# Both low halves of each table block of the first product-key pass on GpSimd, and a larger selection budget per block

## The reference, cut to what matters

```python
def _peer(hn, w_query, sub_keys, expert_down, expert_up):
    q = (hn @ w_query).reshape(b, s, PEER_HEADS, 2, PEER_QUERY_DIM // 2)
    sc = jnp.einsum('bshcd,hckd->bshck', q, sub_keys)
    v1, i1 = lax.top_k(sc[..., 0, :], 16)
    v2, i2 = lax.top_k(sc[..., 1, :], 16)
    cand = (v1[..., :, None] + v2[..., None, :]).reshape(b, s, 8, 256)
    cidx = (i1[..., :, None] * 128 + i2[..., None, :]).reshape(b, s, 8, 256)
    top, pos = lax.top_k(cand, 16)
    idx = jnp.take_along_axis(cidx, pos, axis=-1)
    gate = jax.nn.softmax(top, axis=-1)
    ...
        act = gelu(hb . expert_down[ib]);  out = (gate * act) . expert_up[ib]
```

## Time and profile before

| | |
|---|---|
| median of 3 runs | 4505.56 us (4504.31 to 4511.51) |
| the profiled execution | 4504.23 us, its span 4502.3 us |
| busy in the span | PE 4045.6 us (90%), DVE 3031.9 (67%), ACT 2273.7 (51%), POOL 1127.2 (25%) |
| first pass, by TensorE | 3318.5 to 3955.9 us |
| second pass, by TensorE | 3959.5 to 4497.9 us |
| HBM | 1001.57 MB read, 77.97 MB written |

### The profile page before, as it was taken

One profiled execution on the slowest core, in us unless ns is written; L12 is line 12 of the kernel. 1 busy time (PEld: TensorE's weight loads), 2 busy tenths in 40 slices (PEclk: granted clock), 3 DMA queues, 4 the chain that ended last, 5 costly groups with the idle time before them and its releaser, 6 DMA issues. The chain is left out here.

```text
span 4502.3 us, 60232 instructions
## 1 busy us (share of the span) xinstructions
PE 4045.6 (90%) x22760; PEld 3230.1 (72%) x22760; DVE 3031.9 (67%) x3742; ACT 2273.7 (51%) x2916; POOL 1127.2 (25%) x547
## 2 busy tenths in 40 slices
PE   6797769999999999999699779789879999999999
PEld 6785646666555655555479777678779999988787
DVE  5254468888888888888446342254489877788884
ACT  3332146676676666677335235322335989533332
POOL 2121100000000000000122222132224555666662
PEclk9898879999999999999799889899889999999999
DMA  2222269999999999999423321232236999999995
GB/s 87 66 67 78 69 241 343 362 367 366 363 366 349 364 366 365 364 369 355 151 88 101 137 79 63 91 103 71 89 135 214 318 348 348 355 357 373 355 344 189
DMA packets 506172, 1082.32 MB, mean 240 GB/s; under 512 B 23570, under 2 KB 209170, under 8 KB 494712
## 3 DMA queue, kind: packets, MB, share of 16 engines
q1 hardware_dynamic: 465416, 936.49, 58.4%
q0 software_dynamic: 40560, 143.16, 8.7%
HBM read 1001.57 MB, written 77.97 MB: 240 GB/s over the span
## 5 line engine op out<-in xcount | busy, mean ns | idle before, releaser
L1627 DVE TENSOR_TENSOR ffn_low<-moe_expert_raw,moe_expert_high 128x2048 fp32r<-128x2048 f32 (+1 forms) x576 | 1189.8, 2110 | 255.7 <-ACT moe_expert_high L1580 255.7
L1580 ACT CAST moe_expert_high<-moe_expert_raw 128x2048 fp32r<-128x2048 f32 x570 | 976.0, 1764 | 420.0 <-DMA moe_expert_raw<-in_w_gate 137.3
L2876 ACT CAST peer_high<-peer_raw 128x1024 fp32r<-128x1024 f32 x256 | 256.2, 1050 | 443.4 <-PE peer_ps L2858 265.8
L1473 POOL DMA_INDIRECT scratch_h<-ffn_result,ffn_y_rows x16 | 46.3, 2896 | 1340.7 <-DVE ffn_result L1619 1340.7
L298 PE MATMUL peer_ps<-peerbuf_hnT_high,peer_high 128*128 128x384 f32 x1024 | 353.2, 345 | 27.2 <-DVE peer_low L2682 23.5
L299 PE MATMUL peer_ps<-peerbuf_hnT_high,peer_low 128*128 128x384 f32 x1024 | 344.3, 336 | 0.0
L300 PE MATMUL peer_ps<-peerbuf_hnT_low,peer_high 128*128 128x384 f32 x1024 | 344.2, 336 | 0.0
L2682 DVE TENSOR_TENSOR peer_low<-peer_raw,peer_high 128x1024 fp32r<-128x1024 f32 x192 | 257.0, 1366 | 102.6 <-ACT peer_high L2876 102.2
L298 PE MATMUL ffn_gate_p<-moe_expert_high,ffn_x_high 128*66 128x512 f32 (+1 forms) x768 | 290.2, 378 | 18.8 <-DVE ffn_low L1627 18.8
L298 PE MATMUL ffn_up_p<-moe_expert_high,ffn_x_high 128*66 128x512 f32 (+1 forms) x768 | 288.4, 376 | 5.8 <-DVE ffn_low L1627 5.8
L298 PE MATMUL ffn_down_p<-moe_expert_high,ffn_t_high 128*66 128x512 f32 x704 | 279.4, 397 | 12.5 <-DVE ffn_low L1627 12.5
(11 more groups left out here) (523 smaller groups left out, 10021.9 us busy)
## 6 DMA issues: line engine op xcount, KB each, us to landing
moe_expert_raw<-in_w_gate SPq DMA_DIRECT2D x80, 2048.0 KB, 9.6
moe_expert_raw<-in_w_up SPq DMA_DIRECT2D x80, 2048.0 KB, 9.9
moe_expert_raw<-in_w_down SPq DMA_DIRECT2D x80, 2048.0 KB, 10.7
peer_raw<-in_peer_down_t SPq DMA_DIRECT2D x64, 1024.0 KB
peer_raw<-in_peer_up_t SPq DMA_DIRECT2D x64, 1024.0 KB
scratch_a<-peer_gelu SPq DMA_DIRECT2D x64, 384.0 KB
scratch_g<-peer_spread SPq DMA_DIRECT2D x24, 1024.0 KB
peer_spread<-scratch_g SPq DMA_DIRECT2D x16, 1536.0 KB, 12.3
```

What stands on the lines that cost most here:

```text
L1473: pool.indirect_dma_start(h_dram, bass.IndirectOffsetOnAxis(ap=y_rows[:, 0:1], axis=0), result[:, :], None, compute_op=ALU.add).then_inc(y ...
L1580: act.copy(half_of(high, q, h), half_of(raw, q, h)).then_inc(high_done, 1)
L1627: dve.tensor_tensor(half_of(low, q, h), half_of(raw, q, h), half_of(high, q, h).bitcast(F32), ALU.subtract).then_inc(low_done, 1)
L2876: act.copy(high[:, q % 2, cols], raw[:, q % PR_RAW, cols]).then_inc(high_done, 1)
```

## The change

GpSimd makes both low halves of the blocks of the first pass, and DVE none; the semaphores are counted accordingly (`low_done_pool` counts every half of the first pass, `low_done` those of the second). The budget of a block goes from 6.0 to 7.2, which puts more selection pieces in each block and everything behind them in earlier blocks. The second pass has the same instructions.

```diff
@@ -2487,7 +2487,7 @@
     for b in range(PEER_BLOCKS):
-        budget, many = 6.0, 0
+        budget, many = 7.2, 0
@@ -2684,8 +2684,10 @@
         def lows_made(engine, q):
-            engine.wait_ge(low_done, q + 1 if q < PAIRS else PAIRS + 2 * (q - PAIRS + 1))
-            engine.wait_ge(low_done_pool, min(q + 1, PAIRS))
+            if q < PAIRS:
+                engine.wait_ge(low_done_pool, 2 * (q + 1))
+            else:
+                engine.wait_ge(low_done, 2 * (q - PAIRS + 1))
@@ -2778,8 +2780,8 @@
                 for q in range(PEER_BLOCKS):
-                    if q < PAIRS:
-                        low_half(pool, q, 1).then_inc(low_done_pool, 1)
+                    for half in (0, 1) if q < PAIRS else ():
+                        low_half(pool, q, half).then_inc(low_done_pool, 1)
@@ -2824,7 +2826,7 @@
                         pe.wait_ge(high_done, tile + 1)
-                        pe.wait_ge(low_done if j == 0 else low_done_pool, q + 1)
+                        pe.wait_ge(low_done_pool, tile + 1)
@@ -2936,7 +2938,7 @@
                 for q in range(PEER_BLOCKS):
-                    for half in range(1 if q < PAIRS else 2):
+                    for half in (0, 1) if q >= PAIRS else ():
                         low_half(dve, q, half).then_inc(low_done, 1)
```

## The result

| | before | after |
|---|---|---|
| median | 4505.54 us | 4535.46 us (4531.78 to 4541.3, 4 runs) |
| ratio | | 1.0068 (95% interval 1.0053 to 1.0083) |
| span of the profiled execution | 4502.3 us | 4539.5 us |
| first pass, first to last matmul | 637.4 us | 671.4 us |
| second pass | 538.5 us | 537.6 us |

The change makes the kernel slower by 0.7%, more than my range held (4499 to 4534) and more than twice what I forecast (+13). The 34.0 us in the first pass are nearly the whole of it. Of the 37 us between the two profiles, 2.5 lie ahead of the pass, in code that is the same (DVE's last search step there ends that much later), and 1.1 between that step and the first matmul, which waits for a low half that now takes GpSimd 2.4 us and took DVE 1.2. The runs' medians differ by 30.

The account below looks back on a forecast made before the run. The prediction took DVE to bound the first pass for 190 us and TensorE for 449 us. From 4504.23 us, +4 up to and behind the last one-hot wait, +11 in the tail and -1 in the second pass gave 4518 us, range 4499 to 4534.

Parts of the forecast that it names:

- the last coupled group is 0.9: First pass: the last one-hot group TensorE waits for is 0.9 in block 15, where it was 0.11 in block 19.
- The break-even at 154.4: First pass: group 0.9 ready 154.4 us after the first matmul, with 483.0 us of TensorE work behind it, would break even.
- DVE starts sooner: Start of the first pass: DVE begins with a selection step at about 3309.0 instead of waiting 8.6 us for a cast.
- The stalls, 20 us: DVE up to group 0.9: held up 20 us in all by GpSimd's low halves, ends 9 and 27 us.
- TensorE is free from there: First pass behind group 0.9: DVE's remaining work fits beside some 7 us of TensorE work, so TensorE waits no more.
- Term 2: Tail of the first pass, from block 51: GpSimd needs 10.0 us a block against TensorE's 8.32 and becomes the bound; +11 us.
- Term 3: Second pass: fewer accumulations and an earlier end of full DMA load shorten TensorE's waits; -1 us (-5 to +3).
- B: Rival, first pass: faster, the end of the selection decides alone and stalls stay at 9 us; 4496 us, chance 0.13.
- C: Rival: gathers wait for dots and dots for DMA rows, a ring that delays GpSimd's low halves; 4536 us, chance 0.12.

Follow-up runs that it names:

- e6: The changed kernel with at most two groups in each block up to block 21 (before: three in blocks 16, 18, 20): 4530.64 us, ratio 1.0049.
- e7: The kernel before with GpSimd making both low halves in blocks 0 and 1 alone, budget 6.0: 4504.78 us, ratio 0.9990.
- e5: The changed kernel with GpSimd's half 0 cut to one column instead of 1024 in blocks 2 to 16: 4518.21 us, ratio 1.0024.
- e3: The changed kernel with one wait more: GpSimd waits for the end of half 0 before it begins half 1: 4537.71 us, ratio 1.0067.
- e2: The kernel before with the budget alone raised to 7.2, DVE keeping half 0 of every first-pass block: 4555.99 us, ratio 1.0108.
- e4: The changed kernel with GpSimd making both halves only in blocks 0 to 16, DVE half 0 from block 17: 4530.94 us, ratio 1.0057.

## Why the prediction was wrong

- **That the last coupled group is 0.9**: right. It came at 173.9 us. The break-even at 154.4 took TensorE to be free for the 483.0 us behind it; they were 497.5, and 488.2 in e6.
- **DVE starts sooner**: right. Its first instruction follows the stage before by 0.5 us instead of 8.6. TensorE's first low half comes 1.1 us later, which I had left out. e7 shows that this is worth something only because DVE has no low half left in its order.
- **The stalls, 20 us**: the step that failed. They were 35.7, above my upper end of 27 too. I took a rate per low half (0.63 to 0.79 us) from the old schedule and multiplied it by the new number. The mechanism was right, the rate wasn't: it changes with the schedule, 0.8 us a low half before, 1.1 after, 1.8 with the larger budget alone. The error moves the one-hot by 15.7 us. e5 shows the mechanism by itself: 15 low halves less are 20 us less stall, 19.9 us on the one-hot and 17 us of time. That the low halves come in pairs isn't what made the rate too low: e3 takes the pairs apart and keeps the stall, e2 has no pairs and the highest rate.
- **"TensorE is free from there"**: wrong, a second step. I had seen that ScalarE was within 2 us of DVE, and didn't carry it past the selection. 5.2 us of waits and the slow clock behind them; e6: 7.2 us of the pass in blocks 16 to 21.
- **Term 2, the tail, +11 us**: the mechanism was right, the size wrong. GpSimd's pairs there stand 9.3 to 9.6 us apart (five blocks from 3935.94 to 3982.33, and from 3871.87 to 3919.93), where I had 10.0, and the first accumulations are two rows in block 57 and not three, so TensorE was idle six times, 3.8 us together, 5.4 with the slow restarts; e4: 4.8.
- **Term 3, -1 us**: -0.9 in the profile, which confirms nothing: the second pass takes 533.2 to 540.6 us in the profiles of e4 and e6, with the same instructions.
- **Rivals**: B needed half the stall rate and got more than the old one. C named the right size for a wrong reason, so its hit is luck: no ring through the gathers shows after block 20, DVE and DMA had time there. What I had not asked is what each of the two edits does alone. The larger budget was to me a consequence of the move; it was the costly one (e2).

Sum of the pass: 19.5 on the one-hot, 5.4 in the tail, and the 9.1 left of 34.0 between them.

What stays open: what sets the rate of the stall, and so why e3's sum didn't fall although the waits were cut in two, and why e2's is highest; whether a GpSimd low half can be placed under the search or a reduction at all times, which would cost nothing by these rows, wasn't tried. The longest single wait, the first for a group (10.50 us at 3434.23), I did not take apart further.

## What to carry to other kernels

When two engines share work, it isn't only the load that an engine loses that counts, but what it then waits for: 23 us of low halves left DVE and 20 us of stall came back. A stall rate read from one schedule doesn't carry over to another. Fixed work that bounds a stretch leaves TensorE time for other work beside it; packing it into fewer blocks (here four fewer, 33 us of TensorE) hardly shortens that work and leaves more for afterwards. A planner's parity (here two or three groups in the block behind the selection) was worth 7 us of the pass. Each edit should be costed alone before their sum.

## What the runs showed of the hardware

A DVE instruction with two SBUF inputs that meets a GpSimd low half waits for it, and can wait for two that run back to back: 7.04 us for one of 2.29 us, twice, and once 7.41. If GpSimd first waits for the end of its first one, DVE gets in between (4.74 us), and the next one waits for the second. So the Trainium skill's rule (SBUF — State Buffer, Who interferes with whom), whole instructions excluding each other, holds here.

That two of them count as one for DVE is no rule by these rows: at 3477.14 in the kernel after, DVE got in between two low halves without such a wait (4.48 us). What decides isn't shown.

A one-input reduction kept its 2.28 us in all eight cases, five of them over a GpSimd low half. One input alone doesn't protect, though: a `tensor_scalar` with one input, 0.23 us undisturbed, was held until the end of a chain of four low halves.

```profile
3365.79 9.37 POOL L2682 TENSOR_TENSOR peer_low<-peer_raw,peer_high 128x1024 fp32r<-128x1024 f32 x4
...
3367.90 7.36 DVE L2560 TENSOR_SCALAR peer_part<-peer_pos 128x128 uint32<-128x128 uint32 x1
```
